# Loading expert weights as one 16 KB piece per partition instead of four 4 KB pieces

## What is computed

```python
def clamped_swiglu(h_gate, h_lin):
    h_gate = jnp.minimum(h_gate, SWIGLU_LIMIT)
    h_lin = jnp.clip(h_lin, -SWIGLU_LIMIT, SWIGLU_LIMIT)
    return h_gate * jax.nn.sigmoid(SWIGLU_ALPHA * h_gate) * (h_lin + 1.0)

def moe_ffn(x, router_w, router_b, w_gate, b_gate, w_up, b_up, w_down, b_down):
    # 32 experts, each token goes to its 4 best ones
    ...
    def expert_block(args):
        xb, e = args
        h = clamped_swiglu(xb @ w_gate[e] + b_gate[e], xb @ w_up[e] + b_up[e])
        return h @ w_down[e] + b_down[e]
```

## Time and profile before

| | |
|---|---|
| median of the runs | 1367.33 us |
| span of the profiled execution | 1368.3 us |
| TensorE matmul busy | 1245.1 us (91%), 5895 instructions |
| TensorE weight load busy | 592.5 us (43%) |
| VectorE busy | 411.8 us (30%) |
| ScalarE busy | 282.8 us (21%) |
| GpSimd busy | 46.3 us (3%) |
| DMA | 446.89 MB, mean 327 GB/s over the span |
| chain that ended last | TensorE 59%, DMA 28%, VectorE 4%, SP's queue 4% |

### The profile page before, as it was taken

One profiled execution on the slowest core, in us unless ns is written; L12 is line 12 of the kernel. 1 busy time (PEld: TensorE's weight loads), 2 busy tenths in 40 slices (PEclk: granted clock), 3 DMA queues, 4 the chain that ended last, 5 costly groups with the idle time before them and its releaser, 6 DMA issues.

```text
span 1368.3 us, 16171 instructions
## 1 busy us (share of the span) xinstructions
PE 1245.1 (91%) x5895; PEld 592.5 (43%) x5896; DVE 411.8 (30%) x1070; ACT 282.8 (21%) x501; POOL 46.3 (3%) x38
## 2 busy tenths in 40 slices
PE   7999999999999999999898989898898988898994
PEld 6877885865433333333333333333333333333331
DVE  1652342212323322242222223232222223322225
ACT  0231241121112121222211112112211112112111
POOL 0103200100100000000000000000000000000001
PEclk9999999999799999999999999999999999999998
DMA  8642204328799978999999999999999999999980
GB/s 310 244 162 77 108 13 152 124 76 334 275 362 410 409 291 316 410 409 410 410 410 410 409 410 410 410 410 409 410 410 410 410 409 410 410 410 410 410 359 31
DMA packets 117111, 446.89 MB, mean 327 GB/s; under 512 B 6768, under 2 KB 7744, under 8 KB 117088
## 3 DMA queue, kind: packets, MB, share of 16 engines
q1 hardware_dynamic: 112752, 440.45, 81.3%
q10 hardware_dynamic: 4336, 6.12, 1.3%
HBM read 445.51 MB, written 1.05 MB: 326 GB/s over the span
## 4 chain that ended last, share of the span: by engine, by line
PE 59%; DMA 28%; DVE 4%; SPq 4%; issue 2%; DVEq 2%; POOL 0%; POOLq 0%; ACT 0%; ACTq 0%
DMA main<-in_exp_w_up_dram 27%; PE bank L1247 24%; PE bank L1283 9%; PE bank L827 8%; PE bank L817 5%; SPq L425 3%; PE bank L1180 2%; DMA main<-in_w_in_dram 2%; PE bank L1046 2%; DVEq L1700 1%; PE bank L868 1%; PE bank L958 1%; PE bank L965 1%; PE bank L1270 1%; DVE conv_in L1701 1%
## 5 line engine op out<-in xcount | busy, mean ns | idle before, releaser
L1247 PE MATMUL bank<-main 128*64 128x512 f32 x2112 | 478.1, 612 | 40.6 <-DMA main<-in_exp_w_up_dram 39.7
L1247 PEld LDWEIGHTS bank<-main 128*64 128x64 f32 x2112 | 152.3, 141 | 345.6 <-issue 300.9
L1283 PE MATMUL bank<-main 128*64 128x512 f32 x1056 | 233.9, 594 | 52.4 <-DVE main L1708 52.4
L1698 DVE TENSOR_TENSOR conv_in<-bank,main 128x256 f32<-128x256 f32 x66 | 27.8, 421 | 533.3 <-PE bank L1270 533.3
L1283 PEld LDWEIGHTS bank<-main 128*64 128x64 f32 x1056 | 87.2, 137 | 197.3 <-issue 197.3
L771 ACT ACTIVATE main<-bank 128x512 f32<-128x512 f32 x66 | 39.4, 598 | 441.5 <-PE bank L1247 441.5
L827 PE MATMUL bank<-main 128*128 128x512 f32 x192 | 84.1, 593 | 0.5 <-ACT main L647 0.5
L1675 DVE TENSOR_TENSOR main<-main,bank 128x512 f32<-128x512 f32 x132 | 81.4, 677 | 0.0
L817 PE MATMUL bank<-main 128*128 128x256 f32 x352 | 77.9, 380 | 0.0
L778 ACT ACTIVATE conv_in<-bank 128x512 f32<-128x512 f32 x33 | 19.7, 597 | 264.7 <-PE bank L1283 264.7
L817 PEld LDWEIGHTS bank<-main 128*128 128x128 f32 x352 | 66.3, 190 | 10.2 <-issue 1.5
(11 more groups left out here) (250 smaller groups left out, 930.1 us busy)
## 6 DMA issues: line engine op xcount, KB each, us to landing
main<-in_exp_w_gate_dram SPq DMA_DIRECT2D x64, 2048.0 KB, 21.8
main<-in_exp_w_up_dram SPq DMA_DIRECT2D x64, 2048.0 KB, 23.2
main<-in_exp_w_down_dram SPq DMA_DIRECT2D x64, 2048.0 KB, 21.2
main<-in_w_in_dram SPq DMA_DIRECT2D x7, 2048.0 KB, 27.5
main<-in_xa_wk_dram SPq DMA_DIRECT2D x2, 2048.0 KB, 10.8
main<-in_w_out_dram SPq DMA_DIRECT2D x2, 2048.0 KB, 10.8
main<-in_xa_wv_dram SPq DMA_DIRECT2D x2, 2048.0 KB, 11.3
main<-in_xa_wq_dram SPq DMA_DIRECT2D x2, 2048.0 KB, 13.6
```

Of the source, the lines that this page charges most:

```text
L1247: last = pe.matmul(moe_bank[f][64 * side:64 * side + 64, :], xg_chunk(k), weights(role, k, f), start=(k == 0), stop=(k == KC - 1))
L1283: last = pe.matmul(moe_bank[4][64 * h:64 * h + 64, :], hT[:, k, :], weights(role, k, h), start=(k == 0), stop=(k == KC - 1))
L1698: tt(mg[:, f, :, :], gT[:, :, 0, :], bias(0), ALU.add)
```

## The change

A partition now gets four neighbouring rows of an expert's matrix: of half h of a matrix, partition p gets rows 512h + 4p to 512h + 4p + 3, which lie together in HBM (16 KB). Chunk j of the half then consists of rows 512h + 4p + j. So that the other operand has the same order, each transpose of `gu` and `xg_sb` reads every fourth column (columns 4c + j) instead of 128 neighbouring ones. The biases are loaded as 64 rows of 512 numbers and transposed in 8 pieces of 64 x 128, every fourth column each, and the bias operand of VectorE steps over 64 columns from chunk to chunk. Places, waits and the number of loads stay as they are.

```diff
-        bias_raw = gdn_mem[:, 1536:2048].rearrange("p (w b n) -> p w b n", w=2, b=2)
+        bias_raw = gdn_mem[0:2 * N_EXPERTS, 1024:2048].rearrange("p (w c j) -> p w j c", w=2, j=4)
...
-                w = d[ROLE_INPUT[role]][0, ahead:].rearrange("e (k p) n -> e p k n", p=P)
+                w = d[ROLE_INPUT[role]][0, ahead:].rearrange("e (h p j) n -> e h p (j n)", h=2, j=4)
                 h = (0, 0, 1, 1, 0, 1)[role]
                 at = weights_at(role, odd)
-                dst = main[:, at:at + SLOT_COLS].rearrange("p (k n) -> p k n", k=4)
-                src = w[bass.ds(e, 1), :, 4 * h:4 * h + 4, :].rearrange("e p k n -> p (e k) n")
+                dst = main[:, at:at + SLOT_COLS]
+                src = w[bass.ds(e, 1), h, :, :].rearrange("e p n -> p (e n)")
...
-                act.dma_start(bias_raw[:, w, :, :], d[n][0].rearrange("(b e) (c f) -> (e c) b f", b=2, f=P)).then_inc(ld_bias, 16)
+                act.dma_start(gdn_mem[0:2 * N_EXPERTS, 1024 + HALF * w:1024 + HALF * (w + 1)],
+                              d[n][0].rearrange("e (f c) -> (e f) c", f=2)).then_inc(ld_bias, 16)
...
-                for b in range(2):
-                    last = pe.transpose(ps[:, (2 * w + b) * P:(2 * w + b + 1) * P], bias_raw[:, w, b, :], ident)
+                for j in range(4):
+                    last = pe.transpose(ps[:, (4 * w + j) * 64:(4 * w + j + 1) * 64], bias_raw[:, w, j, :], ident[0:64, 0:64])
...
             def gathered_T(ps):
                 for j in range(4):
-                    last = pe.transpose(ps[:, j * P:(j + 1) * P], xg_sb[:, j * P:(j + 1) * P], ident)
+                    last = pe.transpose(ps[:, j * P:(j + 1) * P], xg_sb[:, :].rearrange("p (c j) -> p j c", j=4)[:, j, :], ident)
...
-                            last = pe.transpose(moe_bank[2 + f][:, j * P:(j + 1) * P], gu[:, f, j * P:(j + 1) * P], ident)
+                            last = pe.transpose(moe_bank[2 + f][:, j * P:(j + 1) * P],
+                                                gu[:, f, :].rearrange("p (c j) -> p j c", j=4)[:, j, :], ident)
...
-                bias4 = [ebias[:, w, :].rearrange("p (e k) -> p e k", k=KC) for w in range(2)]
+                bias4 = [ebias[:, w, :].rearrange("p (j e f) -> p e f j", j=4, f=2) for w in range(2)]
...
-                        b = bias4[w][:, bass.ds(e, 1), 4 * f:4 * f + 4].rearrange("p e k -> p (e k)")
+                        b = bias4[w][:, bass.ds(e, 1), f, :].rearrange("p e j -> p (e j)")
```

## The result

The changed kernel takes 1335.70 us (median of 4 runs, 1334.07 to 1336.26) against 1367.55 us for the kernel before (4 runs, 1365.43 to 1372.65): a ratio of 0.977, with a 95% interval of 0.974 to 0.979. So 31.9 us are gone, where I had forecast no change. The measured time lies inside the range, between the middle and the outer end of the first rival. The profiled execution has a span of 1332.3 us and a time of 1334.07 us, so some 1.8 us lie around a span. The profiled 1368.3 us of before were therefore 2.5 us above their median rather than the 1.0 us that I took, and the two spans differ by 36.0 us.

The account below looks back on a forecast made before the run. The prediction took the expert loads to bound 720.6 us and TensorE the rest. Loads -1.4, transposes +2.2 and biases +0.4 made +1.2 us on the profiled 1368.3 us: 1369.5, or 1368.5 us as a median; range 1333 to 1390 us.

Parts of the forecast that it names:

- Rival 1: Expert loads: each piece has a price beside its bytes, 6.9 ns, -23 us: 1346 us, bounds 1322 and 1363; chance 0.30.
- What bounds the kernel: Whole kernel: TensorE up to 545 us, expert loads from 545 to 1265.57 us (720.6 us), then three blocks of TensorE.
- The loads: Expert loads (L425): 16 KB pieces instead of 4 KB save 0.4 ns per extra piece, -1.4 us of 720.6 us.
- The transposes: Transposes in the loop: strided reads cost 54 ns each, 0.22 us per TensorE-paced block, 10 blocks: +2.2 us, bounds 0 and +6.5.
- The biases: Bias transposes ahead of the loop: eight with half the columns instead of four, once on the path: +0.4 us.
- Rival 2: Transposes in the loop: strided reads are dear, three times 136 ns each: 1384 us; decides from about 170 ns; chance 0.14.
- Rival 3: Expert loads: 16 KB pieces stream worse, 0.77 against 0.64 us, the 720 us grow by 20%: 1512 us; chance 0.06.

Follow-up runs that it names:

- the last experiment: Changed kernel with ScalarE's copies writing the transposes' order: 0.979 of the kernel before; the changed kernel itself, rerun on the same chip: 0.980 (1336.30 against 1364.61 us).

## Why the prediction was wrong

**What bounds the kernel: right, but its stretch was taken too short.** The load rate set 20 blocks, and nearly the whole gain lies there. The prediction's own formula with the right rate gives 720.6 us x (1 - 29.365/30.72) = 31.8 us. But the rate counts from where SP goes on loading after its pause, some 30 us ahead of the 545 us that I took. SP's queue before, then after the change:

```profile
516.32 0.38 SPq L425 DMA_DIRECT2D main<-in_exp_w_up_dram  x1
...
513.65 0.34 SPq L425 DMA_DIRECT2D main<-in_exp_w_up_dram  x1
```

From there to the last block that waits it was 749.25 us and is 715.61 us: 33.6 us less, 4.5%. Traces of one kernel differ there: from the sixth to the last block the changed kernel saves 33.4 us by its first trace and 32.1 us by that of the last experiment. So it is partly luck that 31.8 us meets the 31.9 us between the medians so closely: the formula's stretch is too short, it leaves out the transposes and the biases, and on the chip of the last experiment the medians are 28.3 us apart.

**The loads: wrong, and this is the step that failed.** I put a gain of 1.4 us where, by the same formula, 31.8 us were due. I had a price per piece between 0.4 ns and 13.7 ns and took the lower end, 0.4 ns, where the runs show 9.4 ns, since it "alone is a stream without gaps". It was no such stream. It was 2 us near the end of one load that had started slowly, as the windows of the same load show (61 to 63, 62 to 64, 63 to 65 us, before the change):

```profile
DMA packets 296, 0.61 MB, mean 303 GB/s; under 512 B 0, under 2 KB 0, under 8 KB 296
...
DMA packets 380, 0.78 MB, mean 389 GB/s; under 512 B 0, under 2 KB 0, under 8 KB 380
...
DMA packets 386, 0.79 MB, mean 395 GB/s; under 512 B 0, under 2 KB 0, under 8 KB 386
```

The rate rises from window to window and has no level; 389 GB/s in the second is near the 387 that 2 KB pieces keep up in a stream, and 409 was the highest of the windows that hold 2 KB pieces alone. Why it passes the steady rate for 2 us isn't shown; no run tried it., which count two whole pairs of loads, were nearer: 13.7 against 9.4 ns. I had noted that they also hold the slow starts; whether these are the whole of the difference isn't shown. And the steady 4 KB stream held a warning: it had 409.6 GB/s, while I never asked what kept it from more.

**Rival 1: the mechanism was right, its size too small.** I took half of the upper price, 6.9 ns; it is 9.4 ns. That is 28.2 of 640 ns, 4.4%, instead of 3.2%. The 425 GB/s of the Trainium skill's page "DMA: Bandwidth & Descriptors" (Bandwidth) gave an estimate of 26 us. The runs show 428.5 GB/s.

**The transposes: right in kind, half the size, in fewer blocks.** I took 54 ns more for each and 0.22 us per block that TensorE paces; it is 0.10 us, from 28.02 to 28.12 us. It lies where I had put it, on the first four: the chain of waits has 0.70 us for them where the earlier trace rows has 0.60 us.

```profile
522.03 0.70 PE bank L1271 x4
```

The 54 ns were worked out from an operand that streams past (L1247), while these transposes have their data as the operand that is loaded. Eight of them grew by 0.14 us, though each weight load grew by 70 ns. TensorE's weight-load timeline shows why, before and after:

```profile
524.64 0.86 PEld L1270 LDWEIGHTS bank<-kst,main 128*128 128x128 f32 x8 [0.81 <-issue]
...
521.96 1.04 PEld L1271 LDWEIGHTS bank<-kst,main 128*128 128x128 f32 x8 [0.81 <-issue]
```

Eight loads of 210 ns are 1.68 us and stand in 1.04 us, so they overlap one another, and the 70 ns are what one load gets longer, not what a row of them costs for each.

The cost should count in 7 blocks, not in 10: the 5 ahead of 506 us and the 2 behind the last wait, an estimate of 0.7 us where I had 2.2. In the 9 unwaited distances between them the loads already run with hardly a gap, so what TensorE loses should come off its next wait. The runs don't contradict this, but can't prove it: from the sixth block to the last one that waits, the kernel without the step takes 724.3 us and the changed kernel 722.9 and 724.2 us in two traces, which differ by more than the 0.9 us in question.

Rival 2 needed 170 ns per transpose and got about 20. For it I had leaned on the Trainium skill's page "SBUF — State Buffer" (the note on cachelines). The runs don't bear out its rule for this read: a step of two, with two hits in a line, costs the same 70 ns as a step of four.

**The biases: near.** Eight transposes now take 1.10 us on the path where four took 0.44 us, so +0.7 us instead of +0.4 us; the row of after, from the chain of waits:

```profile
338.57 1.10 PE bank L1126 x8
```

**Rival 3** (16 KB pieces stream worse) is out: 16 KB pieces of the loads start every 0.61 us, so what makes the instruction fetches of the earlier trace rows take 0.77 us and more isn't their length.

## What to carry to other kernels

Where the loads pace the kernel, ask what a piece costs beside its bytes, and choose the mapping of rows to partitions that makes the pieces long; here 4 KB to 16 KB gave 4.6% more rate, with the data order repaired in transposes that were there anyway. Take a price per piece only from a stream that holds its level over many loads; the four windows of 2 us in one load gave 303 to 409 GB/s. A bound from whole loads and one from such a window aren't equal witnesses, and taking the wrong one put the forecast some 30 us off.

## What the runs showed of the hardware

- In a steady stream a DMA piece of 2, 4, 8 or 16 KB takes 9.4 ns plus its bytes at 27.2 B per ns and engine: 387, 410, 422 and 428 GB/s. How far apart a partition's pieces lie in HBM made no difference (2 KB pieces 4 KB or 512 KB apart, 4 KB pieces 8 KB or 512 KB apart), nor did it matter whether 2 KB pieces lie together in SBUF, nor whether 2 MB in 8 KB pieces come in one DMA or two.
- The weight load of a float32 transpose takes 140 ns when it reads neighbouring columns and 209 to 210 ns with a step of two or four; since the loads overlap, eight in a row take 0.86 us and 1.04 us (step of four). ScalarE's copy of 128x512 from PSUM takes 597 ns when it writes neighbouring numbers and 1074 ns when it writes with a step of 128 numbers.
